# Turning the samples' state sums on TensorE and adding over groups on VectorE, in one decoder step with an mLSTM state

## The reference

```
    num = decay[..., None] * jnp.einsum('bhtd,bhdv->bhtv', q, c_prev) + jnp.einsum('bhts,bhsv->bhtv', s, v)
    den = decay * jnp.einsum('bhtd,bhd->bht', q, n_prev) + jnp.sum(s, axis=-1)
    h = num / jnp.maximum(jnp.abs(den), jnp.exp(-m_t))[..., None]
    ...
    c_new = carry[..., None, None] * c_prev + jnp.einsum('bhs,bhsd,bhsv->bhdv', g, k, v)
```

## Time and profile before

| | us |
|---|---|
| median of 3 runs | 1698.96 (1697.58 to 1699.06) |
| the profiled execution's own time | 1698.14 |
| its span, first to last instruction | 1696.4 |
| TensorE busy in it | 1684.1 |
| VectorE busy in it | 1194.5 |
| GpSimd busy in it | 477.6 |

### The profile page before, as it was taken

How to read it: one execution, slowest core, us unless ns; L and a number is a source line. 1 busy time by engine, 2 the same in 40 slices (tenths; PEclk the granted TensorE clock), 3 DMA queues, 4 the chain that set the end, 5 groups by cost and what they waited for, 6 DMA issues and landing times.

```text
span 1696.4 us, 37171 instructions
## 1 busy us (share of the span) xinstructions
PE 1684.1 (99%) x13712; PEld 1677.6 (99%) x13712; DVE 1194.5 (70%) x1901; ACT 767.4 (45%) x916; POOL 477.6 (28%) x501
## 2 busy tenths in 40 slices
PE   9999999999999999999999999999999999999997
PEld 8999999999999999999999999999999999999997
DVE  5875857677585766758688877777555777777554
ACT  6545435353443535344445554544333334334443
POOL 4422415242241524224333222222000222222220
PEclk9999999999999999999999999999999999999999
DMA  8788786868878687877766666666666666566663
GB/s 208 189 223 199 199 212 172 212 176 219 192 190 217 166 216 180 212 192 193 195 180 181 190 178 183 180 180 174 183 183 181 180 179 183 174 184 175 186 178 121
DMA packets 591309, 318.80 MB, mean 188 GB/s; under 512 B 17756, under 2 KB 586060, under 8 KB 589156
## 3 DMA queue, kind: packets, MB, share of 16 engines
q1 hardware_dynamic: 578564, 292.99, 64.0%
q10 hardware_dynamic: 10592, 21.57, 5.1%
q0 software_dynamic: 2064, 2.92, 0.8%
HBM read 305.09 MB, written 12.78 MB: 187 GB/s over the span
## 4 chain that ended last, share of the span: by engine, by line
PE 99%; DMA 0%; ACT 0%; DVE 0%; SPq 0%; issue 0%; ACTq 0%; DVEq 0%
PE strip L1526 32%; PE strip L1530 32%; PE strip L1534 32%; PE aux L1408 1%; PE strip L1457 0%; DMA w_raw<-in_w_in 0%; PE aux L1587 0%; PE aux L1477 0%; PE strip L1470 0%; PE aux L1617 0%; PE aux L1616 0%; PE aux L1630 0%; PE aux L1621 0%; PE aux L1614 0%; PE aux L1622 0%; PE aux L1613 0%
## 5 line engine op out<-in xcount | busy, mean ns | idle before, releaser
L714 ACT ACTIVATE w_hi<-w_raw 128x1024 fp32r<-128x1024 f32 x557 | 588.7, 1060 | 786.1 <-PE strip L1534 753.1
L987 DVE TENSOR_TENSOR w_lo<-w_raw,w_hi 128x1024 fp32r<-128x1024 f32 x556 | 710.3, 1282 | 295.0 <-ACT w_hi L714 292.6
L1526 PE MATMUL strip<-xh,w_hi 128*128 128x268 f32 (+1 forms) x2016 | 291.0, 286 | 0.0
L1530 PE MATMUL strip<-xl,w_hi 128*128 128x268 f32 (+1 forms) x2016 | 290.0, 286 | 0.0
L1534 PE MATMUL strip<-xh,w_lo 128*128 128x268 f32 (+1 forms) x2016 | 290.0, 286 | 0.0
L1526 PEld LDWEIGHTS strip<-xh,w_hi 128*128 128x128 f32 x2016 | 265.1, 188 | 0.2
L1530 PEld LDWEIGHTS strip<-xl,w_hi 128*128 128x128 f32 x2016 | 265.2, 188 | 0.0
L1534 PEld LDWEIGHTS strip<-xh,w_lo 128*128 128x128 f32 x2016 | 265.2, 188 | 0.0
L1526 PE MATMUL strip<-x2h,w_hi 128*128 128x266 f32 x1408 | 200.2, 284 | 0.0
L1530 PE MATMUL strip<-x2l,w_hi 128*128 128x266 f32 x1408 | 199.9, 284 | 0.0
L1534 PE MATMUL strip<-x2h,w_lo 128*128 128x266 f32 x1408 | 199.9, 284 | 0.0
(11 more groups left out here) (330 smaller groups left out, 1525.5 us busy)
## 6 DMA issues: line engine op xcount, KB each, us to landing
w_raw<-in_w_in SPq DMA_DIRECT2D x256, 512.0 KB, 4.5
w_raw<-in_w_up SPq DMA_DIRECT2D x176, 512.0 KB, 4.1
w_raw<-in_w_down SPq DMA_DIRECT2D x64, 512.0 KB, 4.1
w_raw<-in_w_out SPq DMA_DIRECT2D x32, 512.0 KB, 4.7
w_raw<-in_w_down SPq DMA_DIRECT2D x32, 384.0 KB, 3.4
out<-c_st ACTq DMA_DIRECT2D x8, 1024.0 KB, 7.1
c_st<-in_state_mlstm_C ACTq DMA_DIRECT2D x7, 1024.0 KB, 10.8
rb<-scratch_rows ACTq DMA_DIRECT2D x8, 270.0 KB, 5.1
```

Of the source, the lines that this page charges most:

```text
L714: act.activation(w_hi[:, slot, :], w_raw[:, slot, :], ACT.Copy).then_inc(hi_done, 1)
L987: v.tensor_tensor(w_lo[:, slot, :], w_raw[:, slot, :], w_hi[:, slot, :].bitcast(f32), ALU.subtract).then_inc(lo_done, 1)
L1526: pe.matmul(bank[b][:, 0:c1 - c0], w_hi[:, slot, w], rh[:, k0 + k, c0:c1], start=(first and k == 0), stop=False)
L1530: pe.matmul(bank[b][:, 0:c1 - c0], w_hi[:, slot, w], rl[:, k0 + k, c0:c1], start=False, stop=False)
```

## The change

The reduce that makes `sel` goes, and so do the two products with it in each head. In their place TensorE transposes both halves of `sacc` with the identity, each into 128 columns of `aux[0]` and `aux[1]`, behind the denominator's two matmuls instead of ahead of them. VectorE then adds over the 16 groups with two reduces out of PSUM into the small tile `hsum`, waits for its own two reduces, and multiplies `hsum` by the reciprocal where it had multiplied the PSUM columns.

```
-        sel = sb("sel", [P, NS])
+        hsum = sb("hsum", [P, 2, NS])
...
-            v.tensor_reduce(sel[:, :], ident[:, :].rearrange("p (g b) -> p b g", b=NS), mybir.AxisListType.X, ALU.add)\
-             .then_inc(sel_done, 1)
...
                         v.wait_ge(sample_done, n + 1)
-                        v.tensor_tensor(h_t[:, :, PM:NM], aux[0][:, PM:PM + 2 * NS].rearrange("p (a b) -> p a b", a=2),
+                        for w in range(2):
+                            v.tensor_reduce(hsum[:, w, :], aux[w][:, PM:PM + P].rearrange("p (g b) -> p b g", b=NS),
+                                            mybir.AxisListType.X, ALU.add).then_inc(hsum_done, 1)
+                        v.wait_ge(hsum_done, n * 2 + 2)
+                        v.tensor_tensor(h_t[:, :, PM:NM], hsum[:, :, :],
                                         rden[:, PM:NM].unsqueeze(1).broadcast_to([P, 2, NS]), ALU.mult)\
                          .then_inc(hs_step, 1)
...
-                        pe.wait_ge(sel_done, 1)
-                        pe.wait_ge(sacc_step, (n + 1) * (JG + 1))
-                        for w in range(2):
-                            mm = pe.matmul(aux[0][:, PM + w * NS:PM + (w + 1) * NS], sacc[:, 0, w * P:(w + 1) * P],
-                                           sel[:, :], start=True, stop=True)
-                        mm.then_inc(sample_done, 1)
 
                         pe.wait_ge(psum_step, n * PST + PST)
                         pe.matmul(aux[2][:, 0:NM], ones[:, :].bitcast(f32r), p_hi[:, :], start=True, stop=False)
                         pe.matmul(aux[2][:, 0:NM], ones[:, :].bitcast(f32r), p_lo[:, :], start=False, stop=True)\
                           .then_inc(num_done, 1)
+                        pe.wait_ge(sacc_step, (n + 1) * (JG + 1))
+                        for w in range(2):
+                            mm = turn(aux[w][:, PM:PM + P], sacc[:, 0, w * P:(w + 1) * P], P)
+                        mm.then_inc(sample_done, 1)
```

More of the change, by code:

```diff
@@ L329, in hybrid_decoder_step @@
             sem("scores_done"), sem("kv_turned"), sem("kv_done"), sem("vs_done"), sem("v_kept"))
-        wsc_done, qkd_done, qkd_turned, sn_done, sel_done = (
-            sem("wsc_done"), sem("qkd_done"), sem("qkd_turned"), sem("sn_done"), sem("sel_done"))
+        wsc_done, qkd_done, qkd_turned, sn_done, hsum_done = (
+            sem("wsc_done"), sem("qkd_done"), sem("qkd_turned"), sem("sn_done"), sem("hsum_done"))
         psum_step, n_kept = sem("psum_step"), sem("n_kept")
```

## The result

The changed kernel takes **1702.17 us** (median of 11 runs, 1700.15 to 1703.34), the kernel before 1697.60 on the same chip (1697.27 to 1699.30): the ratio is 1.0023, with a 95% interval of 1.0015 to 1.0030. The forecast was 1697.0 and a range of 1695.4 to 1699.0.

The account below looks back on a forecast made before the run. TensorE's own stream was taken as the bound; 0.21 us saved in each of eight heads, 1.7 in all, with VectorE's additions costing nothing, gave 1696.4 to 1697.3, put at 1697.0 us, range 1695.4 to 1699.0.

Parts of the forecast that it names:

- The products that go, the transposes that come: Second block of each head, L1624 to second eight: 1.58 to 1.60 us against 1.80; 0.21 saved, 1.7 in eight heads.
- The step that failed: Ahead of strip 11 in each head: transpose pair costs 0.13 us, plus 0.08 to 0.10 in the strip behind it.
- a wait: In every head TensorE waits for `w_lo` once VectorE adds 5.56 us; at 7 us added, 1709; chance 0.02.
- a longer instruction: Each transpose of the pair holds TensorE for its whole record; the change loses 1.8 us, giving 1700.8; chance 0.03.
- the spread of executions: Whole time: runs 1.48 us apart; lower-edge median less the saving's upper end, 2.4, gives 1695.2; chance 0.07.
- four signs of being wrong: A strip waits for `w_lo`; eight behind the pair far above 1.07 us; clock there below 1.00; PSUM reduces take microseconds.
- VectorE: Two PSUM reduces and a wait add 0.70 us a head ahead of `cgs`; 5.56 us of room, so no cost.
- the third rival: In each head the eight matmuls behind the pair run at 1.2 GHz: 7.8 us more, 1705; chance 0.02.
- The sum: Whole kernel: profiled 1698.14 less 1.7 gives 1696.4, median less 1.7 gives 1697.3; forecast 1697.0 between, range 1695.4 to 1699.0.

Follow-up runs that it names:

- run 3: The kernel before with TensorE unchanged, plus the two reduces and their wait on VectorE, sums unused: 1697.44 us against 1698.79, ratio 0.9997.
- Experiments 2: The kernel before with its two `sel` products moved behind the denominator's two matmuls, no transposes or reduces: 1702.52 us, ratio 1.0025.
- the fillers in the kernel before: The kernel before with one rounded matmul of 8 to 240 columns directly ahead of strip 11 in heads 1 to 7: 1700.49 us in one run.
- 1: The changed kernel with the two transposes ahead of the denominator's two matmuls instead of behind: 1704.37 us against 1698.79 for the kernel before, ratio 1.0039.
- 4: The changed kernel with five more transposes of `sacc` directly ahead of its two, seven in a row: 1703.98 us in one run.
- orders 2 and 3: The changed kernel, one transpose either side of the denominator's matmuls, or both ahead of the state product's seven: 1696.25 and 1696.59 us against 1697.62 before.
- 5: The changed kernel with extra transposes or rounded matmuls varied by head, one trace repeated: 1703.12, 1702.69, 1702.27, 1702.48 us against 1697.21 before.

## Why the prediction was wrong, point by point

- *The products that go, the transposes that come*: right in place. 1.58 to 1.60 us was forecast, 1.59 measured, so 0.21 saved where it stands. The sum was right as a sum of the instructions that change, in part by luck: the first eight took 1.09 (194.47 - 193.38) instead of 1.05 to 1.07, and the matmuls ahead of it some 0.03 less than forecast.
- **The step that failed**: "a pair costs its 0.13 and some 0.08 to 0.10 that the strip behind it pays." It took for granted that the strips behind then run on at their old pace. They ran at 0.993 instead of 0.977, in the 35 eights behind the first 0.58 us a head, almost three times the saving. No rival had this either: they looked for a wait, a longer instruction, a lower clock or the spread of executions. None of the four signs of being wrong that the prediction names came, so they could not have told of it. The runs show that this pace is the cause of the longer heads: a filler of 8 columns, or another order of the same instructions, brings it back to 0.977 with the change left in (heads of 99.43 and 99.33 us).
- It could have been asked from the trace of before, which has both paces. Strip 4, behind the strips of 280 columns, runs at 0.993 in every head, in heads 1 to 7 with nothing but strips ahead of it:

```profile
148.07 1.16 PE L1530 MATMUL strip<-xl,w_hi 128*128 128x268 f32 x8
149.07 1.16 PE L1534 MATMUL strip<-xh,w_lo 128*128 128x268 f32 x8
```

  Head 0 has both behind its first block. At first:

```profile
57.59 1.14 PE L1526 MATMUL strip<-xh,w_hi 128*128 128x268 f32 x8
58.56 1.14 PE L1530 MATMUL strip<-xl,w_hi 128*128 128x268 f32 x8
```

  and, one transpose of `tails` later (the program has it in head 0 alone), at the same shape:

```profile
64.59 1.16 PE L1530 MATMUL strip<-xl,w_hi 128*128 128x268 f32 x8
65.58 1.15 PE L1534 MATMUL strip<-xh,w_lo 128*128 128x268 f32 x8
```

  These are 0.97 and 0.99 by the starts. I compared only the first eight behind a block with 0.97 and not the ones that follow.
- *VectorE*: right. A reduce out of PSUM takes 0.28 us, the lower end of what was given (0.29) and not the 0.38 of the reduce out of SBUF that I took; 0.54 us are added instead of 0.70, and the room behind them was enough: alone they cost nothing (run 3).
- *The clock*: the third rival did not come. The strips at 0.993 stand in a stretch at the upper level: the granted clock is 1.00 from 193 to 196 us.
- *The sum*: eight heads give 2.9 us more instead of 1.7 less. The base was off as well: the forecast starts from a median of three runs, 1698.96, where eleven give 1697.60; and its range begins at 1695.4, though it was to take in 1695.2. The rest of the 4.1 us between the two spans is 0.4 at the start, before the first head (last section), 0.4 in the last projection, where the strips between the pairs of transposes take 114.77 us instead of 114.36, and 0.36 in the last steps, where VectorE's reciprocal starts later behind ScalarE's root. That last one is in this row, with 0.70 us of idle time where the kernel before has 0.34:

```profile
1691.51 0.17 DVE L1007 RECIPROCAL rfs<-rfs 128x3 f32<-128x3 f32 x1 [0.70 <-ACT rfs L962]
```

  Experiments 2 and 3 and the fillers in the kernel before, which keep `sel`, do not have it; the kernels without `sel` do, in all the traces compared. Why was not tried.

What stays open: what in TensorE keeps the two paces, and what settles which of them a stretch gets; no run separates the moment of entry from anything else that the order of earlier work leaves behind. The runs exclude the kind of the instruction directly ahead (1, 4), the number of instructions alone (changed kernel against orders 2 and 3, 37146 in each), VectorE's work (2, which is slow without the reduces, and 3), and chance from one execution to the next (the repeated trace in 5).

## What to carry to other kernels

Where a dense stream of matmuls is the path, an edit's price is what it takes in place plus what it does to the pace of everything behind it; read the distance of starts in the strips before and after the place, not just in it, and look whether the trace of before already has two paces for one shape. If it has, try the same edit in several orders, one to a loop pass that is written out, in one run: here that turned heads of 99.91 us into heads of 99.33, where before they took 99.54. A small result in such a kernel tells little on the idea until its place has been varied.

## What the runs showed of the hardware that I had not expected

- Eight matmuls of 128 x 128 with 268 columns, weights loaded for each, have two lasting paces at the same granted clock: 0.977 and 0.993 us. Which one a stretch gets is fixed by the program, as far as two traces of one kernel show (5), and it can change at a place whose instructions did not change (1, 4).
- Behind the two transposes a matmul of 8 columns holds the stream for 0.11 us (192.89 to 193.00), nearly as much as one of 268, 0.12. In the kernel before, directly behind L1636, it takes 0.03 (192.67 to 192.70), and the eight behind it 1.08.
- At the start, the changed kernel's trace has a stretch at a mean clock of 0.57, so part of it at 1.2 GHz, behind a stretch in which TensorE was busy for 1.64 of 2 us. The trace of before has none, though TensorE was busy for only 1.15 of the same 2 us there, so these rows do not tell what makes the clock fall:

```profile
10.00:12.00 2.00, 1.64 (x10) 1.17 (x10) 2.00 (x6) 1.49 (x4) 0.00 (x0) 1.00 1.16 276
12.00:16.00 4.00, 4.00 (x23) 3.97 (x22) 3.79 (x8) 2.46 (x6) 2.38 (x1) 0.57 1.13 265
```

  Its first head starts at 53.31 us, against 52.91 before. Of the 18 traces here, five have such a stretch, and their first heads start at 53.29 to 54.34 us; in the others it is 51.35 to 52.91. The programs differ, so what of these 3 us belongs to the execution is not separated; two traces of one kernel (5) are 0.08 us apart. But the changed kernel's own eleven executions point the same way: the five with a mean granted clock of 0.998 took 1700.15 to 1701.59 us, the six with 0.996 or 0.997 took 1702.17 to 1703.34. So part of the 4.6 us between the two medians may be the start and not the change, and heads are the safer thing to compare.
